# Two fillers of 32 bytes in a decoder layer's SBUF layout: the weight tiles move by 32 bytes, the placed tiles by 64

## The reference, cut to what matters

```python
h = rmsnorm(x, norm_mix_g)
u_pool, q, k, v, f_logit, g_logit = split(h @ w_in)                # 1024 x 4104
y_pool = pool_mixer(u_pool, pool_w, pool_scale) @ w_pool_out
y_fox = forgetting_attention(q, k, v, f_logit + b_forget) @ w_fox_out   # 8 heads of 64, causal
x = x + (g_pool * y_pool + g_fox * y_fox) @ w_out
x = x + memory_cross_attention(rmsnorm(x), rmsnorm(mem), w_xq, w_xkv, w_xo)  # 4 heads of 128, 256 memory tokens
x = x + (silu(gt) * up) @ w_ffn_out, with gt, up = rmsnorm(x) @ w_ffn_in     # 1024 -> 2 x 2816 -> 1024
return rmsnorm(x, norm_final_g)
```

## The kernel before

| tiles | start | modulo 64 | modulo 512 |
|---|---|---|---|
| `w_raw0`, `w_raw1` | 8320, 12416 | 0 | 128 |
| `w_hi0` to `w_hi2`, `w_lo0` to `w_lo2` | 16512 to 36992, every 4096 | 0 | 128 |
| `ident`, `ident_r`, `mask`, `mask_r` | 41088 to 42624, every 512 | 0 | 128 |
| small tiles `ss` to `x_inv` | 43136 to 44448 | 0 or 32 | mixed |
| every placed tile (`h_*`, `d_*`, `z_*`, `o_*`, `hx_*`, `hf_*`, `late_*`, `s2_*`, `t2_*`, `q*`, `k1*`, `prob`, ...) | 44576 + kb x 1024 (+ 2048 inside some) | 32 | 32 |

## Time and profile before

### The profile page before, as it was taken

One profiled execution on the slowest core, in us unless ns is written; L12 is line 12 of the kernel. 1 busy time (PEld: TensorE's weight loads), 2 busy tenths in 40 slices (PEclk: granted clock), 3 DMA queues, 4 the chain that ended last, 5 costly groups with the idle time before them and its releaser, 6 DMA issues.

```text
span 1548.3 us, 18589 instructions
## 1 busy us (share of the span) xinstructions
PE 1495.4 (97%) x7268; PEld 1215.2 (78%) x7268; DVE 896.6 (58%) x1226; ACT 557.0 (36%) x987; POOL 378.4 (24%) x311
## 2 busy tenths in 40 slices
PE   6999999999999999999999799999999999999996
PEld 5778888787787888888777678888888888888785
DVE  4172522566665423326563766677677777778966
ACT  5223311555644312116442452222222221444444
POOL 4000000000000000205001664444444443348202
PEclk9999999999999999999999899999999999999998
DMA  7333355631210352513210222222222222883333
GB/s 182 54 44 55 70 81 73 104 53 18 55 28 28 71 80 78 222 41 96 81 42 28 109 69 102 103 102 102 102 102 103 102 102 106 310 297 91 108 95 130
DMA packets 103399, 147.79 MB, mean 95 GB/s; under 512 B 4744, under 2 KB 69768, under 8 KB 101904
## 3 DMA queue, kind: packets, MB, share of 16 engines
q1 hardware_dynamic: 94288, 117.72, 29.4%
q0 software_dynamic: 4464, 15.77, 2.9%
q10 hardware_dynamic: 4560, 13.11, 2.2%
HBM read 113.78 MB, written 32.80 MB: 95 GB/s over the span
## 4 chain that ended last, share of the span: by engine, by line
PE 89%; DVE 5%; POOL 2%; ACT 2%; DMA 1%; issue 1%; SPq 0%; POOLq 0%; DVEq 0%; ACTq 0%
PE ps L1552 27%; PE ps L1554 27%; PE ps L1553 27%; PE ps L1802 2%; PE ps L1751 2%; PE ps L1782 1%; DVE t_lo L1053 1%; DMA w_raw<-in_w_in 1%; PE ps L1783 1%; DVE s_lo L1053 1%; POOL w_lo L516 1%; PE ps L1559 0%; POOL rstd L508 0%; PE ps L1994 0%; DVE hf_lo_B L1053 0%
## 5 line engine op out<-in xcount | busy, mean ns | idle before, releaser
L1042 DVE TENSOR_TENSOR w_lo<-w_raw,w_hi 128x1024 fp32r<-128x1024 f32 (+1 forms) x58 | 70.5, 1216 | 245.7 <-ACT w_hi L656 243.8
L1552 PE MATMUL ps<-h_lo,w_hi 128*128 128x512 f32 (+1 forms) x456 | 184.3, 404 | 6.6 <-POOL w_lo L516 4.7
L1554 PE MATMUL ps<-h_hi,w_lo 128*128 128x512 f32 (+1 forms) x456 | 180.1, 395 | 0.0
L1553 PE MATMUL ps<-h_hi,w_hi 128*128 128x512 f32 (+1 forms) x456 | 180.0, 395 | 0.0
L656 ACT ACTIVATE w_hi<-w_raw 128x1024 fp32r<-128x1024 f32 (+1 forms) x66 | 69.4, 1051 | 299.6 <-PE ps L1554 284.1
L1552 PE MATMUL ps<-t_lo,s_hi 128*128 128x512 f32 x308 | 120.3, 390 | 2.0 <-DVE t_lo L1053 1.5
L1554 PE MATMUL ps<-t_hi,s_lo 128*128 128x512 f32 x308 | 119.9, 389 | 0.0
L1553 PE MATMUL ps<-t_hi,s_hi 128*128 128x512 f32 x308 | 119.8, 389 | 0.0
L1552 PEld LDWEIGHTS ps<-h_lo,w_hi 128*128 128x128 f32 x456 | 87.0, 191 | 25.9 <-POOL w_lo L516 4.9
L1554 PEld LDWEIGHTS ps<-h_hi,w_lo 128*128 128x128 f32 x456 | 86.9, 191 | 20.1
L1553 PEld LDWEIGHTS ps<-h_hi,w_hi 128*128 128x128 f32 x456 | 87.1, 191 | 18.1
(11 more groups left out here) (303 smaller groups left out, 3673.5 us busy)
## 6 DMA issues: line engine op xcount, KB each, us to landing
w_raw<-hs_dram SPq DMA_DIRECT2D x77, 256.0 KB, 2.7
w_raw<-in_w_in SPq DMA_DIRECT2D x33, 512.0 KB, 8.1
raw_p<-in_w_ffn_in SPq DMA_DIRECT2D x22, 512.0 KB, 4.6
w_raw<-in_w_ffn_in SPq DMA_DIRECT2D x22, 512.0 KB, 4.2
hs_dram<-h_sum SPq DMA_DIRECT2D x11, 1024.0 KB, 8.9
hs_dram<-hq SPq DMA_DIRECT2D x11, 768.0 KB, 7.0
wq_B<-in_w_ffn_out SPq DMA_DIRECT2D x8, 1024.0 KB, 8.0
x_in<-in_x SPq DMA_DIRECT2D x8, 512.0 KB, 9.8
```

What stands on the lines that cost most here:

```text
L1042: nc.vector.tensor_tensor(w_lo[n % SLOTS][:, 0:w], w_raw[n % RAWS][:, 0:w], w_hi[n % SLOTS][:, 0:w].bitcast(FP32), ALU.subtract).then_inc( ...
L1552: nc.tensor.matmul(dst, w_h, x_l, start=start, stop=False)
L1553: nc.tensor.matmul(dst, w_h, x_h, start=False, stop=False)
L1554: return nc.tensor.matmul(dst, w_l, x_h, start=False, stop=stop)
```

## The change

Two tensors that nothing reads or writes are allocated: 8 float32 (32 bytes) per partition ahead of `w_raw`, and the same behind the small tiles, ahead of what `place` counts from. The kept tiles move up by 32 bytes, the placed ones by 64. After it the slots start at 16544 + 4096 i (32 modulo 64, 160 modulo 512) and the placed tiles at 44640 + kb x 1024 (32 modulo 64, 96 modulo 512).

```diff
@@ -138,6 +138,7 @@
                 return st.enter_context(nc.sbuf_tensor(name, shape, dt))
 
 
+        keep("line_fill", [P, 8])
         w_raw = [keep(f"w_raw{i}", [P, 1024]) for i in range(RAWS)]
         w_hi = [keep(f"w_hi{i}", [P, 1024], F32R) for i in range(SLOTS)]
         w_lo = [keep(f"w_lo{i}", [P, 1024], F32R) for i in range(SLOTS)]
@@ -163,6 +164,7 @@
         x_nmax = keep("x_nmax", [P, XH, T])
         x_sum = keep("x_sum", [P, XH, T])
         x_inv = keep("x_inv", [P, XH, T])
+        keep("line_fill2", [P, 8])
 
 
         h_hi = place("h_hi", 0, [P, KD, S], F32R)
```

## The result

| | before | after |
|---|---|---|
| median | 1549.94 us (5 runs, 1546.94 to 1550.54) | 1540.96 us (5 runs, 1539.23 to 1542.33) |
| ratio | | 0.9949, 95% interval 0.9936 to 0.9963 |
| span of the profiled execution | 1548.3 us | 1539.2 us |

The change makes the kernel faster: by 9.0 us or 0.6% between the medians, by 0.5% by the ratio. The kernel before is the less steady of the two, since it sometimes gets less clock: in 17 more runs of it the granted share went from 0.993 (1544.8 to 1545.2 us) to 0.989 (1550.4 to 1550.6 us). The direction was forecast and the time lies in the stated range, but the likeliest case said 1525 us: of the 24.8 us that it summed up, a little over a third came.

What follows compares the result with a forecast made beforehand. PE was taken as the bound, busy 97% of the span, so time is matmul count times start-to-start interval. Terms 3.9 + 1.6 + 2.5 + 17.5 - 0.7 = 24.8 us off 1550.1 gave 1525 us; range 1518 to 1552.

Steps and rivals of the forecast that it cites:

- the likeliest case: Full gain over all slot matmuls: 24.8 us off, 1525 us, own range 1518 to 1530, chance 0.64.
- the two classes: 512-column float32r matmuls: operands differing modulo 64 start every 234.3 or 233.4 ns, agreeing ones every 226.6 ns.
- term 4: Remaining slot-stationary matmuls, outside attention and slack stretches: 2277 x 7.7 ns = 17.5 us gained.
- The unit is 128 bytes or more: Rival: slot pairs differing by 64 still clash, PE keeps 234 ns, 1550 us; no change had chance 0.20.
- term 3: Stretches 0 to 65 and 700 to 920 us: 5.0 us faster matmuls, half lost to waits, 2.5 counted.
- term 6: 256-column matmuls and 128-column transposes with `ident`: nothing gained; 4.7 us more as far end if transposes gain.
- Slower: Rival: unit 128 bytes, price grows with distance, half a line apart is worst; 1565 us, chance 0.09.
- Half the gain: Rival: runs over the slots never settle, staying at 230.0 ns; 15 us less slack, 1537 us, chance 0.07.
- 1. slot moving, bound stretches: Slot-moving matmuls outside 700 to 920 us: 576 x 6.8 ns = 3.9 us gained.
- Term 2: Attention, 300 to 505 us: 375 matmuls in bursts of 12, staying unsettled, 4.3 ns each, 1.6 us gained.
- Term 5: Restarts: some 20 longer runs each begin unsettled for 11 matmuls, taking 0.7 us off the gain.
- Terms 7 and 8: DMAs into shifted `w_raw` (far end 1.2 us) and DVE and ACT work on shifted tiles (9.4 us, DVE): both taken as 0.

Runs made afterwards that it cites:

- ts_128: On top of `d0_p0`, the t2 tiles and those sharing the second FFN product with them lie 128 bytes higher: 1526.79 us.
- d0_p0: Kernel before with only the second filler, at 96 bytes; slots and placed tiles agree, starts at multiples of 128: 1521.87 us, ratio 0.9832.
- d0_p32: Kernel before with first filler 32 bytes, second 96; slots and placed tiles agree, starts 32 past a multiple of 64: 1522.05 us, ratio 0.9835.
- d64_p0: Kernel before with only the second filler, at 32 bytes; slots 64 from placed tiles, starts at multiples of 64: 1541.08 us, ratio 0.9956.

## Why the prediction was wrong

**What failed** is the step from the two classes to the new layout: "All matmul operands then agree modulo 64", and from this that the slot matmuls join the 226.6 ns class. The prediction itself said that the rows couldn't tell the unit, since the trace has only distances of 96 and 0 modulo 512, and gave 0.64 to the full gain on a hint: one cycle in excess for every 16 columns, hence 64 bytes. The hint was a coincidence of numbers, or at least no sign of this period. Measured, the distances 0 and 256 are fast and 32, 64, 96 and 128 slow, so the period is 256 bytes as far as distances were tried, and 64 is a clash like 96. In the sum it is term 4 that falls with this step: 17.5 us forecast, 3.3 us measured.

**The rivals.** "The unit is 128 bytes or more" was right in its cause and wrong in its time: it took the price of the clash to be the same at 64 as at 96 and said 1550 us. The price has a shape: at +64 it is 0.9 ns less than at +96, at -64 about 4 ns less than at -96. That gives, from the table, 3080 x 0.9 + 816 x 4.3 = 2.8 + 3.5 = 6.3 us; the rest of the 9 us is mostly granted clock (about 1.3 us of term 4 below and up to 1.8 us of term 3) and a shorter pace of matmuls with 256 columns (term 6). "Slower" supposed a price that grows with the distance; it doesn't, 128 costs less than 96. "Half the gain" came near the time by another mechanism. The Trainium skill's page "TensorE: Matmul & The Clock Gate" (What happens when you issue a matmul) gives TensorE two independent read ports, so that loading the next weights takes nothing from the running matmul. The prediction read it so that no relation of addresses could matter, and in that reading it isn't borne out: `ts_128` and `d0_p0` differ in nothing but where tiles lie, and the pace of the second FFN product differs by 5.7 ns. Which access hinders which, these runs don't settle.

**The terms.** The sum was made for operands that agree, and `d0_p32` makes them agree; so it can be tested there. I compared its intervals with those of the kernel before one by one (both have the same 7268 matmuls in the same order):

| term | forecast, us | `d0_p32`, us | changed kernel, us |
|---|---|---|---|
| 1. slot moving, bound stretches | 3.9 | 3.7 | 2.4 |
| 2. attention | 1.6 | 1.2 | 0.0 |
| 3. slack stretches | 2.5 (of 5.0) | 4.7 | 3.0 |
| 4. slot stationary, the rest | 17.5 | 18.0 | 3.3 |
| 6. short matmuls, and waits before them | 0 | 0.3 | 0.7 |
| sum with the small remainder | 24.8 | 28.3 | 9.5 |

Term 4 is the one that collapsed: 1.4 ns a matmul in place of 7.7, and only 2.0 of its 3.3 us come from intervals under 245 ns, 0.9 ns each; the other 1.3 us are the eight matmuls on the slow clock at 294 us (1.5) less a longer wait near 1322 us (0.3). They are in `d0_p32`'s 18.0 too, with 1.0 us. In term 3 the waits gave nothing back: I had counted half away, and nearly all came. In `d0_p32` 3.8 of the 4.7 us come from intervals under 245 ns; the rest mixes waits and clock. In the changed kernel 1.8 of the 3.0 us are in longer intervals, and the clock was 0.98 of full speed in 700 to 920 us where the earlier trace rows have 0.96. Term 2 was nearly right where the operands agree: in the bursts of 12 the intervals under 245 ns average 230.2 ns, where the kernel before has 233.4. Term 5's restarts fit as well: 17.0 us came from term 4's intervals under 245 ns, where 17.5 were forecast without restarts.

That 256-column matmuls and transposes wouldn't gain from agreement (term 6) holds, but term 6 missed something. Durations don't show it (`mt_hi,w_hi` has 283 ns with D = 0, where the earlier trace rows have 281); the starts do.

```profile
L1555 PE MATMUL ps<-mt_hi,w_hi 128*128 128x256 f32 x32 | 9.1, 283 | 0.0
```

The first 48 `mt_` matmuls of 256 columns over the slots, 47 intervals at full clock, start so in the kernel before and in the changed one:

```profile
705.57 0.28 PE L1552 MATMUL ps<-mt_lo,w_hi 128*128 128x256 f32 x1
...
711.15 0.28 PE L1554 MATMUL ps<-mt_hi,w_lo 128*128 128x256 f32 x1
...
701.16 0.28 PE L1554 MATMUL ps<-mt_lo,w_hi 128*128 128x256 f32 x1
...
706.51 0.28 PE L1556 MATMUL ps<-mt_hi,w_lo 128*128 128x256 f32 x1
```

That is 5.58/47 = 118.7 ns before and 5.35/47 = 113.8 in the changed kernel (113.7 in `d64_p0` too), while `d0_p32` has 5.63/47 = 119.8 with its operands in agreement. So at 256 columns +64 is the fastest distance tried and agreement no better than a clash. Over the 96 `mt_` matmuls that is 0.5 us, most of the 0.7 in the last row but one.

Terms 7 and 8 hold too. DVE is busy 899.4 us where it was 896.6, ACT 557.0 in both. In the page of the changed kernel the loads into `raw_p` and `w_raw` take 4.6 and 4.2 us as in the earlier trace rows, although both destinations moved, so their difference wasn't the start's.

```profile
raw_p<-in_w_ffn_in SPq DMA_DIRECT2D x22, 512.0 KB, 4.6
w_raw<-in_w_ffn_in SPq DMA_DIRECT2D x22, 512.0 KB, 4.2
```

## What to carry to other kernels

When a trace shows two paces for the same form of matmul, list the start addresses of both operands and compare their difference, not each one's own alignment; here a second filler of 96 bytes in place of 32 makes three times the gain (1522 in place of 1541 us). And when all samples of a trace share one difference, the trace can't give the period: a filler of another size is a one-line experiment, and the forecast should treat the period as unknown. For 512 columns the safe choice is the longest period that the runs allow: put tiles that meet in a matmul at the same remainder modulo 256 or more. For 256 columns measure it anew, since agreement brought nothing there. And before a gain of a few microseconds is put down to a change, see whether both traces had the same clock in the same places.

## What the runs showed of the hardware that was not expected

- 512-column float32r matmuls in a row, each with its own weight load, start every 226.7 ns at full clock if stationary and moving operand start at the same remainder modulo 256 bytes of a partition, and every 229 to 234 ns if not. It isn't the slots: two other kinds of tile, 128 bytes apart in `ts_128`, have 232.4 ns.
- The price depends on the sign of the difference (64: 233.3 ns; -64: 229.1 or 230.1), is 6.4 ns already at 32 bytes (7.3 at 96), and is the same whether the starts are multiples of 64 or not.
- After clashing matmuls the pace needs about 11 more to settle (230.0 ns, then 226.7).
- With 256 columns the order is another: 119.8 ns if the operands agree, 118.7 at 96, 113.8 at 64.
- The kernel before lost about 1.5 us to 1.2 GHz at 294 us in its trace, the changed kernel nothing there, after the same waits.
- Distances below 32 bytes, and other types than float32r, weren't tried.
